# Two halves of a doubling level run together, with one piece of twelve gate instructions in place of two of six

## The reference

```python
def rwkv7_mixer(p, shift_prev, s_prev, ...):
    ...
    def step(s, inp):
        r_t, w_t, k_t, v_t, a_t, b_t = inp
        sa = jnp.einsum('nhvk,nhk->nhv', s, a_t)
        s = (s * w_t[:, :, None, :] + sa[..., None] * b_t[:, :, None, :]
             + v_t[..., None] * k_t[:, :, None, :])
        return s, jnp.einsum('nhvk,nhk->nhv', s, r_t)
    s_last, y = lax.scan(step, s_prev.astype(F32), seq)
    ...
gates = jax.nn.sigmoid(gate_logits).reshape(n, l, N_BRANCH, D_MODEL)
```

## Time and profile before

| | |
|---|---|
| time, median of 3 runs | 2260.98 us (2257.7 to 2262.88) |
| the profiled execution, its own time | 2259.44 us |
| its span, first to last instruction | 2257.7 us |
| TensorE busy | 2180.0 us (97%) |
| VectorE, ScalarE, GpSimd busy | 1154.0, 406.3, 161.9 us |

### The profile page before, as it was taken

One profiled execution on the slowest core, in us unless ns is written; L12 is line 12 of the kernel. 1 busy time (PEld: TensorE's weight loads), 2 busy tenths in 40 slices (PEclk: granted clock), 3 DMA queues, 4 the chain that ended last, 5 costly groups with the idle time before them and its releaser, 6 DMA issues.

```text
span 2257.7 us, 42337 instructions
## 1 busy us (share of the span) xinstructions
PE 2180.0 (97%) x18743; PEld 1615.2 (72%) x18743; DVE 1154.0 (51%) x1773; ACT 406.3 (18%) x783; POOL 161.9 (7%) x276
## 2 busy tenths in 40 slices
PE   6998999999999999999899998999999999999998
PEld 4665666666566566666556687888888888888887
DVE  5875344252353253344234657656663366657654
ACT  3125121232142142142110003111100011111001
POOL 2620000001002002001000000000000000000000
PEclk8999999999999999999999999999999999999999
DMA  8310132201111111021235322111112311111201
GB/s 302 107 43 10 56 127 96 85 9 53 48 49 59 46 51 56 20 81 36 70 129 205 105 77 76 38 39 40 45 67 89 125 40 39 39 39 53 109 29 78
DMA packets 117540, 161.55 MB, mean 72 GB/s; under 512 B 15890, under 2 KB 87047, under 8 KB 117344
## 3 DMA queue, kind: packets, MB, share of 16 engines
q1 hardware_dynamic: 101568, 132.68, 18.1%
q10 hardware_dynamic: 10992, 15.21, 1.9%
q0 software_dynamic: 4800, 10.97, 1.5%
HBM read 126.24 MB, written 32.59 MB: 70 GB/s over the span
## 4 chain that ended last, share of the span: by engine, by line
PE 94%; DVE 2%; ACT 1%; issue 1%; SPq 1%; DMA 0%; DVEq 0%
PE ps L821 93%; PE ps L825 1%; ACT Y L1865 1%; DVE arena L2167 1%; SPq L515 1%; DVE Y L2170 0%; SPq L532 0%; DMA arena<-in_state_s_dram 0%; DVE Y L2167 0%; ACT arena L1763 0%; DVE arena L2621 0%; DVE arena L2367 0%; ACT hT L2071 0%; ACT L1865 0%; DVE Y L2754 0%
## 5 line engine op out<-in xcount | busy, mean ns | idle before, releaser
L821 PE MATMUL ps<-hT,W 128*128 128x352 f32 (+1 forms) x3472 | 1013.4, 442 | 9.8 <-issue 5.2
L821 PEld LDWEIGHTS ps<-hT,W 128*128 128x128 f32 x3472 | 645.8, 191 | 268.6 <-issue 22.5
L821 PE MATMUL ps<-arena 64*64 64x64 f32 (+5 forms) x8888 | 410.8, 244 | 29.8 <-issue 12.0
L821 PEld LDWEIGHTS ps<-arena 64*64 64x64 f32 (+3 forms) x8888 | 325.6, 140 | 157.8 <-issue 83.0
L821 PE MATMUL ps<-arena,W 128*128 128x264 f32 x1200 | 278.2, 386 | 1.6 <-DVE arena L2167 1.6
L821 PEld LDWEIGHTS ps<-arena,W 128*128 128x128 f32 x1200 | 227.9, 190 | 41.1 <-issue 2.1
L2167 DVE TENSOR_TENSOR Y<-Y,ps 128x528 f32<-128x528 f32 x150 | 105.7, 704 | 276.6 <-PE ps L821 276.1
L2167 DVE TENSOR_TENSOR arena<-arena 128x1056 f32<-128x1056 f32 (+7 forms) x164 | 146.7, 894 | 58.1 <-PE ps L821 43.7
L1763 ACT ACTIVATE Y<-ps 128x528 f32<-128x528 f32 (+1 forms) x96 | 39.9, 415 | 747.9 <-PE ps L821 394.1
L821 PE MATMUL ps<-Y,W 128*128 128x352 f32 (+1 forms) x592 | 166.0, 437 | 4.0 <-DVE Y L2167 4.0
L821 PEld LDWEIGHTS ps<-Y,W 128*128 128x128 f32 x592 | 112.8, 191 | 52.7 <-DVE Y L2167 5.0
(11 more groups left out here) (313 smaller groups left out, 1502.5 us busy)
## 6 DMA issues: line engine op xcount, KB each, us to landing
W<-in_w_up_dram SPq DMA_DIRECT2D x22, 1024.0 KB, 7.1
W<-in_w_ada_dram SPq DMA_DIRECT2D x8, 2048.0 KB, 10.3
W<-in_w_in_dram SPq DMA_DIRECT2D x13, 1024.0 KB, 6.8
gates<-arena ACTq DMA_DIRECT2D x72, 176.0 KB, 1.8
arena<-xres SPq DMA_DIRECT2D x22, 528.0 KB, 5.1
arena<-gates SPq DMA_DIRECT2D x21, 528.0 KB, 3.6
xres<-arena POOLq DMA_DIRECT2D x16, 528.0 KB, 7.2
W<-in_w_ada_dram SPq DMA_DIRECT2D x32, 256.0 KB, 2.8
```

The source lines that it names most:

```text
L821: return nc.tensor.matmul(out, lhsT, rhs, start=start, stop=stop, skip_group_check=True)
```

## The change

On TensorE a level becomes `zx` of both halves, one piece of six gate matmuls (twelve instructions), and then `xt_turned` and `yy` of half 0 and of half 1; within a half `xt_turned` now stands ahead of `yy`. On VectorE both additions to `X` stand ahead of both copies to `XT`. Nothing is added or taken out; the matmuls, their operands and their banks are the same.

```diff
@@ tensor
                 for l in range(1, last):
+                    zx(l, 0)
+                    zx(l, 1)
+                    k = 3 * KT + 6 * (l - 1)
+                    gates(k, k + 6)
                     for s in range(2):
-                        zx(l, s)
-                        k = 3 * KT + 3 * (2 * (l - 1) + s)
-                        gates(k, k + 3)
-                        yy(l + 1, s)
                         xt_turned(l, s)
+                        yy(l + 1, s)
                 zt(last, 0)
@@ vector
                 for l in range(1, LEVELS):
+                    last = LEVELS - 1
+                    for s in range(2) if l < last else ():
+                        dve.wait_ge(sem("zx_done"), 8 * j + 2 * (l - 1) + s + 1)
+                        x = X[:].rearrange("p (a s c) t -> p s a (c t)", a=2, s=2)[:, s]
+                        step(tt(x, ps[:, 2 * s:2 * s + 2, 256:512], x, ADD), "zx_ev")
                     for s in range(2):
-                        if l < last:
-                            dve.wait_ge(sem("zx_done"), 8 * j + 2 * (l - 1) + s + 1)
-                            x = X[:].rearrange("p (a s c) t -> p s a (c t)", a=2, s=2)[:, s]
-                            step(tt(x, ps[:, 2 * s:2 * s + 2, 256:512], x, ADD), "zx_ev")
                         dve.wait_ge(sem("zt_done"), level_at(j, l, s))
```

More of the change, by code:

```diff
@@ L1352, in _ @@
                 for l in range(1, last):
+                    zx(l, 0)
+                    zx(l, 1)
+                    k = 3 * KT + 6 * (l - 1)
+                    gates(k, k + 6)
                     for s in range(2):
-                        zx(l, s)
-                        k = 3 * KT + 3 * (2 * (l - 1) + s)
-                        gates(k, k + 3)
+                        xt_turned(l, s)
                         yy(l + 1, s)
-                        xt_turned(l, s)
                 zt(last, 0)
```

## The result

The changed kernel takes 2277.11 us (median of 4 runs, 2276.25 to 2278.12) against 2260.18 before. The ratio is 1.0069, 95% interval 1.0052 to 1.0087: 16.9 us slower. The direction was as forecast; the time lies above the stated range, and the loss is more than twice the 7.0 us of the forecast.

The account below looks back on a forecast made before the run. TensorE, busy 97% of the span, was taken as the bound. Four stretches at +1.82 us plus 0.47 give 7.75, less 0.7 of "issue" time: +7.0, a median of 2268.0 us, range 2263 to 2273.

Parts of the forecast that it names:

- The direction and the mechanism: Four stretches: slower, by new TensorE waits of 0.68 us before the second `xt_turned` and 0.52 before the second `zx`.
- The saving on switches: Each level has one change from 64x64 work to gates and back fewer: 0.37 us, 16 levels, 5.9 us.
- the first rival: Switches are saved and hand-overs hidden in the stretches: 9.4 us less, 2251.6 us; chance 0.07.
- the 2.46 us at which the change begins to lose: Sum of new waits in a stretch above which the change loses; the prediction counted 4.28.
- The hand-over behind ScalarE: From ScalarE's end to TensorE's next matmul: 0.15 us, read at the copy of `W0`.
- 2.14 + 0.71 + 0.60 + 0.15 = 3.60: When `zx(l+1, 1)` starts, in us from `xt_turned(l, 0)`, after the copy of `yy(l+1, 1)`; new wait 0.52.
- The unknown: "Issue" idle time in the stretches, without a releaser: part may vanish, 0 to 2.8 us, 0.7 taken.
- the held cases: Whole time: the forecast's own cases, +4.9 to +9.5 us, 2264.5 to 2271.5 with scatter; chance 0.73.
- The third rival: Clock falls after new waits in the stretches: some 9 us added, 2277 us; chance 0.06.
- Costed at nothing: VectorE's paired additions, weight pieces let go by `zx_done`, ScalarE's saves: no added time.
- H: The prediction's own theory: TensorE waits at hand-overs that nothing covers; 7.3 us forecast in the four stretches.
- F: Theory after the result: most of the loss is "issue" idle time, which dense small work meets more often.

Follow-up runs that it names:

- The shorter copy: Changed kernel with each VectorE copy of `xt_turned` to `XT` cut to half of its columns: 2266.99 us, ratio 1.0036.
- the other order: Changed kernel with steps ordered `xt_turned` 0, `yy` 0, `yy` 1, `xt_turned` 1, `zx` 0, `zx` 1: 2266.98 us, ratio 1.0036.
- the gate in between: Changed kernel with one of each six gate matmuls moved between `yy(l+1, 0)` and `xt_turned(l, 1)`: 2264.79 us, ratio 1.0024.
- the kernel with more of them: Kernel before with each piece of three gate matmuls split in two and one, 32 more changes there and back: 2271.4 us, ratio 1.0056.
- the changed kernel with 32: Changed kernel with 32 more 64x64 matmuls at its very start: 2282.09 us, ratio 1.0091.
- The repeated profile: Changed kernel run once more, unedited: 2275.48 us, ratio 1.0067; the profiled execution took 2275.68 us.
- the three paddings: Kernels before and changed with 0, 16 or 32 matmuls at the start: before 2259.03, 2261.81, 2264.95 us; changed 2275.48, 2274.66, 2282.09 us.

## Why the prediction was wrong

- **The direction and the mechanism** were right. The second `xt_turned` waits for VectorE's copy out of banks 4 and 5, the second `zx` for ScalarE's copy, `zt(5, 0)` for VectorE's. The shorter copy, the other order and the gate in between each took away what was computed for the wait they touch.
- **The saving on switches**, 0.37 us each, was right (0.35 in the windows of the kernel with more of them, 12.0 us against 11.8 in its time). So the first rival failed by its own price: the waits in a stretch were above the 2.46 us at which the change begins to lose.
- **The hand-over behind ScalarE was mis-sized.** The step "2.14 + 0.71 + 0.60 + 0.15 = 3.60" measured 3.74: `yy` starts at 2.15, ScalarE 0.73 later, and from the end of its copy (1081.83) to TensorE's matmul (1082.09) it took 0.26 where the only row before that showed such a step, ScalarE's copy of `W0`, gave 0.15. With the other roundings a level took 0.17 more. Over the stretches 10.0 us were lost net in place of 7.3. Why this hand-over takes 0.26 was not tried. It is not ScalarE as such: behind its 128x352 instructions it was 0.15 too.
- **The step that failed is "The unknown"**: "Where TensorE now stands waiting anyway, part of that may vanish." The bounds 0 and 2.8 us allowed only a gain, and 0.7 of it went into the sum; new "issue" time came only into the upper end of the held cases, as much again in one stretch. The "issue" time grew instead, by 4.0 us in the mean of four profiles each. It stands where a packet of instructions comes too late, at a fixed grid of the list, and mostly where the list ahead of it ran off fast; the change doubled the runs of small matmuls from 96 to 192 rows between gates, and so the places that meet one. That it would also reach the entry was not seen: with `zx(1, 1)` moved there, row 4247 stands in small work, and the first profile of the changed kernel shows 1.83 us of "issue" ahead of it, where the kernel before had gate matmuls. Luck had no part in the direction: the waits in the stretches alone outweigh the saving.
- **The third rival** came true once in the first profile: 1.7 us on one piece of gates. The prediction had argued from single waits under half of 1.60; it was two of them, 0.44 and 1.39, with 0.46 us of work between. The same happened once in the changed kernel with 32: behind 0.43 and 1.20 us a piece of twelve took 5.51 us, with a granted clock of 0.70 over it. The repeated profile had 0.45 and 1.11 at the first of these places, its clock stayed at 1.00, and its time was nearly the same, so the fall isn't needed for the loss.
- **Costed at nothing**: VectorE's order cost nothing (0.9998), and no wait for the modulation weights or for bank 7 appeared.

The sum with the measured terms: 10.0 from the four stretches, 0.5 from `zx(1, 1)` in the second, 4.0 from "issue", 14.5 us, against 16.5, 12.9 and 17.1 measured under the three paddings (mean 15.5). So H carries two thirds of the loss, and F, which put most of it on "issue" time, about a quarter. The last microsecond or so is open. Open too is why some packets come so late: in the kernel before, that of row 13289 started when TensorE had stood for 0.8 us; with 32 matmuls in front, that of row 852 when it had stood for 1.8.

## What to carry to other kernels

Filler work between dependent steps is worth more spread out than in one piece: a switch between tile shapes and back cost 0.35 to 0.37 us, but each hand-over that the second piece had covered put the next step off by 0.66 to 0.68. Before joining two pieces, list every step that then has only steps of its own kind behind it, and take its start-to-start time with the copy from a place in the trace where it is uncovered. Idle time booked as "issue" at equal distances in the instruction list is here time in which instructions are being loaded; it is a cost of dense small instructions, and grew when they were made denser. It is worth setting such times beside the packets of the instruction queue. A change of a few us has to be compared under more than one placement of the list, and with the granted clock of each run beside its time.

## What the runs showed of the hardware

- TensorE's instructions come in packets of 16 KB, one for about 125 matmul rows of these kernels (each with a weight load of its own). In 180 places of 14 profiles TensorE stood until 1.18 to 1.61 us behind the end of a packet, up to 4.5 us at one place, mostly where the 64 rows ahead were started within some 1.6 us.
- 16 and 32 matmuls of padding where TensorE waits anyway made the kernel before 2.8 and 5.9 us slower. A wait of 1.54 us near 148 us of the span became 4.30 and 4.18 us, and the mean granted clock over the 10 us from there fell from 1.00 to 0.66 and 0.83.
- A wait of 0.44 us and one of 1.39, with 0.46 us of work between, were followed by a piece of gates at a mean granted clock of 0.69; 0.45 and 1.11 us at the same place were not.
- In the changed kernel ScalarE's hand-over to TensorE, from the end of its instruction to the next matmul, was 0.14 to 0.15 us behind its 128x1024 and 128x352 instructions and 0.26 (once 0.32) behind the ten of 128x512 ahead of `zx`; VectorE's behind its 128x512 instructions was 0.15.
